# Layer 0 begun on half of the features' modulation, the value projection first in each layer, and a rotation by shuffle

## What is computed

```python
c_act = jax.nn.silu(c)
for l in range(DEPTH):                                  # 2 layers, x is 256 x 1024
    mod = c_act @ w_ada[l] + b_ada[l]                   # 1024 -> 3 x 1024
    shift, scale, gate = split(mod)
    h = rms_norm(x, g_pre[l]) * (1.0 + scale) + shift
    (cq, ckv, kr, za, qb_, kb_, vb_, zb, qc, kc, vc, zc, gcols) = split_cols(h @ w_in[l], IN_SPLITS)
    ...                                                 # three attention branches, gates, output projections
    x = x + gate * rms_norm(y, g_post[l])
# second block
q_rot = axial_rope(q, row_pos, col_pos)                 # x1*cos - x2*sin, x1*sin + x2*cos, halves of 16
k_rot = axial_rope(k, row_pos, col_pos)
...
x = x + gt2 * rms_norm_2(ec_moe(h2, ...))               # 16 experts, each 3 x 1024 x 2752 weights
```

## Time and profile before

| | |
|---|---|
| median of 3 runs | 2330.5 us (2327.39 to 2331.14) |
| profiled execution | 2329.22 us, span 2327.4 us |
| PE busy | 1809.7 us (78%) |
| DVE, ACT, POOL busy | 523.9, 287.3, 61.8 us |
| moved | 714.39 MB, mean 307 GB/s |

### The profile page before, as it was taken

One profiled execution on the slowest core, in us unless ns is written; L12 is line 12 of the kernel. 1 busy time (PEld: TensorE's weight loads), 2 busy tenths in 40 slices (PEclk: granted clock), 3 DMA queues, 4 the chain that ended last, 5 costly groups with the idle time before them and its releaser, 6 DMA issues.

```text
span 2327.4 us, 23978 instructions
## 1 busy us (share of the span) xinstructions
PE 1809.7 (78%) x10388; PEld 1019.3 (44%) x10388; DVE 523.9 (23%) x1136; ACT 287.3 (12%) x710; POOL 61.8 (3%) x101
## 2 busy tenths in 40 slices
PE   6999999999999999989666566656665666666666
PEld 3877785877785677545222222212221222222222
DVE  1144322144323347743000010000100000000001
ACT  1122201122211112311000000000000000000001
POOL 1000000000002100100000000000000000000000
PEclk9999999999999999999777787877787877788787
DMA  9664543445554331388999999999999999999996
GB/s 302 196 203 173 210 147 101 150 163 181 213 180 145 111 124 45 127 331 350 428 426 427 428 429 427 426 430 428 428 425 429 427 427 427 429 427 428 428 428 273
DMA packets 126224, 714.39 MB, mean 307 GB/s; under 512 B 11545, under 2 KB 16089, under 8 KB 96303
## 3 DMA queue, kind: packets, MB, share of 16 engines
q1 hardware_dynamic: 117568, 697.07, 73.9%
q10 hardware_dynamic: 6279, 9.88, 1.4%
q0 software_dynamic: 2272, 5.90, 1.2%
HBM read 709.02 MB, written 3.80 MB: 306 GB/s over the span
## 4 chain that ended last, share of the span: by engine, by line
PE 49%; DMA 44%; DVE 3%; SPq 1%; ACT 1%; issue 1%; POOL 0%; DVEq 0%; ACTq 0%
DMA arena<-in_w_up_dram 22%; DMA arena<-in_w_down_dram 21%; PE banks L832 14%; PE banks L2546 5%; PE banks L1722 4%; PE banks L920 4%; PE banks L1731 3%; PE banks L928 2%; PE banks L2578 2%; DMA arena<-in_w_mods_dram 2%; PE banks L2586 2%; PE banks L837 2%; PE banks L948 1%; PE banks L1764 1%; PE banks L888 1%; PE banks L976 1%
## 5 line engine op out<-in xcount | busy, mean ns | idle before, releaser
L2546 PE MATMUL banks<-arena 128*32 128x512 f32 (+2 forms) x3072 | 418.6, 682 | 330.6 <-DMA arena<-in_w_up_dram 330.6
L2546 PEld LDWEIGHTS banks<-arena 128*32 128x32 f32 x3072 | 131.4, 132 | 588.5 <-issue 580.9
L832 PE MATMUL banks<-arena 128*128 128x256 f32 x1536 | 343.4, 380 | 0.0
L832 PEld LDWEIGHTS banks<-arena 128*128 128x128 f32 x1536 | 287.3, 190 | 39.7 <-issue 3.0
L2578 PE MATMUL banks<-arena 128*32 128x512 f32 x1280 | 206.9, 798 | 92.4 <-DMA arena<-in_w_down_dram 92.4
L2674 DVE SCALAR_TENSOR_TENSOR arena<-arena,banks 64x512 f32<-64x512 f32 (+1 forms) x48 | 30.5, 635 | 519.1 <-ACT arena L2597 518.1
L2578 PEld LDWEIGHTS banks<-arena 128*32 128x32 f32 x1280 | 44.6, 133 | 228.7 <-DMA arena<-in_w_down_dram 128.4
L2597 ACT ACTIVATE arena<-banks 64x512 f32<-64x512 f32 (+1 forms) x48 | 26.7, 556 | 821.1 <-PE banks L2546 819.8
L1722 PE MATMUL banks<-arena 128*128 128x256 f32 x512 | 113.7, 380 | 1.4 <-DVE arena L2119 0.7
L1722 PEld LDWEIGHTS banks<-arena 128*128 128x128 f32 x512 | 95.9, 190 | 16.1 <-issue 3.8
L2681 DVE COPY arena<-banks 128x512 f32<-128x512 f32 x16 | 11.1, 692 | 348.6 <-PE banks L2587 348.6
(11 more groups left out here) (334 smaller groups left out, 1691.1 us busy)
## 6 DMA issues: line engine op xcount, KB each, us to landing
arena<-in_w_gate_dram SPq DMA_DIRECT2D x60, 2752.0 KB, 35.7
arena<-in_w_up_dram SPq DMA_DIRECT2D x60, 2752.0 KB, 32.7
arena<-in_w_down_dram SPq DMA_DIRECT2D x64, 2048.0 KB, 32.4
arena<-in_w_in_dram SPq DMA_DIRECT2D x68, 1024.0 KB, 7.5
arena<-in_w_mods_dram SPq DMA_DIRECT2D x48, 1024.0 KB, 7.4
arena<-in_w_down_dram SPq DMA_DIRECT2D x32, 1024.0 KB, 27.0
arena<-in_w_out_dram SPq DMA_DIRECT2D x12, 1024.0 KB, 5.4
arena<-in_w_gate_dram SPq DMA_DIRECT2D x8, 1376.0 KB, 10.2
```

Of the source, the lines that this page charges most:

```text
L832: mm = pe.matmul(b[:, i * S:i * S + S], w, rhs[:, kt, :], start=kt == 0, stop=kt == 7)
L2546: mm = pe.matmul(bank[pc][32 * g:32 * g + 32, 0:w_], xsT[:, kt, CAP * e4:CAP * e4 + CAP], (wg if g < 2 else wu)[:, c:c + w_], start=kt == ...
```

## The change

- **Half of the features first.** Of layer 0's modulation, blocks 0 and 2 (shift and scale of the features 0 to 511) are made as before. Blocks 1 and 3 are no longer products: VectorE multiplies each row tile by its entry of c and adds, four steps of 128x512 per load (`MODS_B`), and PE adds over the partitions by eight thin products with ones. PE transposes x early into four other banks, without modulation (`turned`). hT's tiles 0 to 3 are written first, and PE makes the first four of eight steps of `vc`, `cq` and the latent keys; the rest of them follows when tiles 4 to 7 are there.
- **Order.** In both layers `vc` is the first job, then `cq`, then the latent keys, which now go to bank SB[0] with signals of their own; the loads are ordered accordingly.
- **Transfers.** x is loaded by SyncE, ahead of the modulation weights. The constants come in two parts: the angle tables of the first rotation are a load of ScalarE's own between the copies of `vc` and `cq`. GpSimd loads the bias tables when VectorE has summed all of `MODS_B`; the T5 product stands between the second halves of `cq` and of the latent keys, `bias_tables(0)` behind the first `qb`.
- **Between the layers.** x of the first half of the tokens is transposed ahead of the last `wout` job, and `vc` begins before the second half of the tokens is scaled; its transposes stand behind seven of the eight steps of the first `vc` job. Fillers go.
- **Second block.** `rk` and `rq` go. VectorE swaps the halves by a shuffle within 32 partitions, and the sine table carries the sign. `gate2` stands ahead of `tq`.

```diff
-    chunk("w_in", D, 0, 416)
+    for r in (0, 512):
+        loads.append(("w_in", r, 4, COL["vc"], 512))
+        loads.append(("w_in", r, 4, 0, 416))
...
-FIRST_MODS = [("ada", 0), ("ada", 1), ("modT", 0), ("ada", 2), ("modT", 1), ("ada", 3), ("modT", 2), ("modT", 3)]
+FIRST_MODS = [("ada", 0), ("ada", 2), ("modT", 0), ("modT", 2)]
...
+MODS_A, MODS_B = (0, 1, 2, 3), (5, 6, 8, 9)
+EARLY = {0: 4, 1: 7}
...
+            sp.dma_start(xv, A["x"][0].rearrange("(t p) d -> p t d", p=P)).then_inc(x_in, 16)
+            for n, turn in enumerate(MODS_A):
+                first_mods(turn, (0, 2)[n // 2], n % 2)
+            load(0, 0)
+            first_mods(MODS_B[0], 1, 0)
+            sp.wait_ge(job_done.sem, made(0, FIRST_MODS.index(("ada", 0)) - PRE))
+            first_mods(MODS_B[1], 1, 1)
+            load(0, 1)
+            sp.wait_ge(job_done.sem, made(0, FIRST_MODS.index(("ada", 2)) - PRE))
+            first_mods(MODS_B[2], 3, 0)
+            first_mods(MODS_B[3], 3, 1)
...
+                if l == 0:
+                    front, back = range(4), range(4, 8)
+                    x_columns(0, 1)
+                    diff_values(0, front)
+                    x_columns(0, 2)
+                    diff_values(1, front).then_inc(part_done.sem, part_done.up())
+                    latent_queries(front)
+                    latent_keys(front).then_inc(part_done.sem, part_done.up())
+                    for n in range(2):
+                        pe.wait_ge(sum_read.sem, sum_read.at(0, 2 * n + 2))
+                        for i in range(4):
+                            mm = pe.matmul(mod_cols[:, 4 * n + i:4 * n + i + 1], th[:, 512 * n + i * P:512 * n + i * P + P],
+                                           ones[:, 0:1], start=True, stop=True)
+                    mm.then_inc(part_done.sem, part_done.up())
+                    x_columns(0, 3)
+                    diff_values(0, back)
+                    x_columns(0, 4)
+                    diff_values(1, back)
+                    latent_queries(back)
+                    pe.wait_ge(tables_in, 160)
+                    pe.matmul(MB[0:12, :], TAB[0:33, 0:12], T5[0:33, :], start=True, stop=True).then_inc(pro_pe.sem, pro_pe.up())
+                    latent_keys(back)
+                else:
+                    x_columns(l, 2)
+                    diff_values(0, range(7))
+                    for hf in range(2):
+                        turned(l, 1, hf)
+                    diff_values(0, range(7, 8))
+                    x_columns(l, 4)
+                    diff_values(1, range(8))
+                    latent_queries(range(8))
+                    latent_keys(range(8))
...
                 act.wait_ge(lam_sum.sem, lam_sum.at(l, 1))
                 nc.scalar.activation(lam[:, 2:4], lam[:, 0:2], ACT.Exp).then_inc(lam_exp.sem, lam_exp.up())
+                for t in range(2):
+                    j = JOB_OF["vc", t]
+                    copy_job(j, vcv[:, t, :], bank_of(l, j))
+                if l == 0:
+                    act.dma_start(cst[:, ANGLES:NCONST[0]], A["consts"][:, ANGLES:NCONST[0]]).then_inc(const_in, 16)
                 j = JOB_OF["cq", 0]
                 copy_job(j, cq, bank_of(l, j))
                 act.dma_start(row_b, A["b_ada"][l:l + 1, 2 * D:3 * D].to_broadcast([P, D])).then_inc(rows_in, 16)
                 act.dma_start(row_g, A["g_post"][l:l + 1, :].to_broadcast([P, D])).then_inc(rows_in, 16)
-                j = JOB_OF["ckv", 0]
-                act.wait_ge(job_done.sem, made(l, j))
-                nc.scalar.copy(ckv, bank_of(l, j)[:, 0:S])
+                act.wait_ge(ckv_done.sem, ckv_done.at(l, 1))
+                nc.scalar.copy(ckv, SB[0][:, 0:S])
...
+            pool.wait_ge(sum_read.sem, sum_read.at(0, 4))
             pool.dma_start(TAB[0:33, 0:12], A["t5_tab"]).then_inc(tables_in, 16)
...
+            for n, turn in enumerate(MODS_B):
+                s_, acc = turn % RING, th[:, 512 * (n // 2):512 * (n // 2) + 512]
+                dve.wait_ge(ring_full[s_], 16 * (turn // RING + 1))
+                for k in range(4):
+                    w, cond = ring[:, s_, 512 * k:512 * k + 512], cav[:, 4 * (n % 2) + k, 0:1]
...
+                        ins = nc.vector.scalar_tensor_tensor(acc, w, cond, acc, ALU.mult, ALU.add)
...
+                    if j == NJOB - 1 and l + 1 < LAYERS:
+                        for hf in range(2):
+                            turned(l + 1, 0, hf)
...
-    jobs += [("rk", n, ()) for n in range(2)] + [("nv", n, i["vn"]) for n in (2, 3)]
-    jobs += [("tq", n, i["qn"]) for n in range(2)] + [("gate2", n, ()) for n in range(2)]
-    jobs += [("rq", n, ()) for n in range(2)]
+    jobs += [("nv", n, i["vn"]) for n in (2, 3)]
+    jobs += [("gate2", n, ()) for n in range(2)] + [("tq", n, i["qn"]) for n in range(2)]
...
+                    nc.vector.stream_shuffle(half, raw, SWAP).then_inc(own2.sem, own2.up())
+                    nc.vector.tensor_tensor(turned, view(raw, 2, S), two(C("cosna")), ALU.mult)
+                    dve.wait_ge(own2.sem, own2.last())
+                    nc.vector.tensor_tensor(tmp, tmp, two(C("sinna")), ALU.mult).then_inc(own2.sem, own2.up())
+                    dve.wait_ge(own2.sem, own2.last())
+                    nc.vector.tensor_tensor(turned, turned, tmp, ALU.add).then_inc(turned2.sem, turned2.up())
```

More of the change, by code:

```diff
@@ L245, in shape_constants @@
     parts["half"] = np.full((P, 4), -0.5, np.float32)
-    later["rot128"] = rotation(P, 16)
+    parts["cos32"] = np.concatenate([cos, cos] * 4).astype(np.float32)
+    parts["sin32"] = np.concatenate([-sin, sin] * 4).astype(np.float32)
     invd = np.float32(10000.0) ** (-np.arange(0, 32, 2, dtype=np.float32) / np.float32(32))
@@ new lines, in _ @@
+            first_mods(MODS_B[0], 1, 0)
[5 more added lines that the diff above has]
+            first_mods(MODS_B[3], 3, 1)
+            for l in range(LAYERS):
+                for i in range(2 if l == 0 else 0, NLOAD):
+                    if l == 0 and i < 8:
+                        if turn_of(0, i) - RING in MODS_B:
+                            sp.wait_ge(sum_read.sem, sum_read.at(0, MODS_B.index(turn_of(0, i) - RING) + 1))
+                        else:
+                            sp.wait_ge(part_done.sem, part_done.at(0, 1 if turn_of(0, i) - RING == EARLY[0] else 2))
+                    elif i - RING in GATE_LOADS:
@@ L1284, in _ @@
                                             ALU.add).then_inc(reader(0, j), 1)
-                if (kind, c) == ("modT", 0):
-                    for t in range(2):
-                        x_mean(0, t)
-                    for t in range(2):
-                        x_scale(0, t)
+            dve.wait_ge(lv_in, 16)
+            for c in (0, 2):
+                j = FIRST_MODS.index(("modT", c)) - PRE
+                dve.wait_ge(reader(0, j), taken(0, j))
+            first_half(0, mcols[:, 0:48].rearrange("p (a b c) -> p a b c", a=2, b=8)[:, :, 0:4, 0])
+            for n, turn in enumerate(MODS_B):
[3 more added lines that the diff above has]
+                    w, cond = ring[:, s_, 512 * k:512 * k + 512], cav[:, 4 * (n % 2) + k, 0:1]
+                    if n % 2 == 0 and k == 0:
+                        ins = nc.vector.tensor_scalar(acc, w, cond, None, ALU.mult)
+                    else:
+                        done = sum_read if k == 0 else sum_own
+                        dve.wait_ge(done.sem, done.last())
+                        ins = nc.vector.scalar_tensor_tensor(acc, w, cond, acc, ALU.mult, ALU.add)
+                    done = sum_read if k == 3 else sum_own
+                    ins.then_inc(done.sem, done.up())
+            dve.wait_ge(part_done.sem, part_done.at(0, 3))
+            first_half(1, view(mod_cols, 2, 4))
             for l in range(LAYERS):
@@ L1525, in _ @@
                         gated(l, t, c, j)
+                        if t == 1 and l + 1 < LAYERS:
+                            dve.wait_ge(ab_ready.sem, ab_ready.at(l + 1, 1))
+                            for hf in range(2):
+                                x_column(l + 1, 0, hf, hf + 1)
                     dve.wait_ge(ysq.sem, ysq.at(l, 2 * t + 2))
@@ L1537, in _ @@
                     x_scale(l + 1, t)
+                if l + 1 < LAYERS:
+                    for hf in range(2):
+                        x_column(l + 1, 1, hf, hf + 3)
                 leave("dve")
```

304 lines of the change are left out of this document (161 added, 143 removed).

## The result

The changed kernel takes **2309.33 us** (median of 4 runs, 2307.18 to 2313.62) against 2329.36 (4 runs, 2327.39 to 2331.14) on the same chip: the ratio of after to before is 0.9920, 95% interval 0.9908 to 0.9932, so 20.0 us faster. The forecast was 2318, range 2305 to 2325. The profiled execution took 2310.95 us with a span of 2309.1, against 2329.2 and 2327.4 before: 18.3 us between the two spans.

The account below looks back on a forecast made before the run. TensorE's chain was taken to bound the kernel until about 1100 us, then the expert weight stream. Layer 0 +1.3, hand-over +6.2 and second block +4.2 sum to 11.7 us: 2318 us against the 2330.5 median, range 2305 to 2325.

Parts of the forecast that it names:

- the hang: Start of layer 0: ScalarE's second load held until 11.1 us behind the T5 write's issue; norm product 8.0 later; chance 0.42.
- rival 1: Start of layer 0: ScalarE's loads pass as in layer 1, gain 21.8 us, time 2308.7; chance 0.27.
- 1.7 of slow clock: Layer 0, behind the held load: 1.7 us counted for TensorE's slow clock after 9 us of idleness.
- Rival 2: Start of layer 0: only ScalarE's third load waits, for 4 us, no slow clock; 5.6 better than forecast, 2312; chance 0.17.
- B: Time at which the back half of layer 0's start begins on TensorE: forecast 40.2 us, bounds 37.5 and 42.
- rival 3: TensorE stays at 1.2 GHz through layer 0's front half, perhaps the queries' products too: 2333 to 2345; chance 0.05.
- The bias rows: Layer 0's first attention step: scores come before the skewed bias load has landed, VectorE stalls; -1.6 us (0 to -3).
- the hand-over: Between the layers: early transposes, and values begun before the second half of x is scaled; +6.2 us (4 to 7).
- the second block's start: Shuffle for rotation products, gate products ahead of queries: scores 4.1 us behind queries instead of 8.25; +4.2 (2 to 5).
- rival 4: Bias load late by the whole 12.6 us, or T5 tables miss their 2.6: up to 4 us more, 2322; chance 0.09.
- one for one: From about 1100 us the expert weight stream's length is fixed by bytes, so time saved before it moves the end equally.
- from there on both traces must be parallel: After the hand-over between the layers, both traces keep their distance, the expert stretch as long as before to 1 us.

Follow-up runs that it names:

- run 5: Changed kernel with ScalarE's two broadcast row loads issued between the key copies and the squares; 2318.54 us, ratio 0.9960 to the kernel before.
- Run 2: Changed kernel with five idle products of 256 columns on TensorE around the second four thin products; 2312.20 us, ratio 0.9927 to the kernel before.
- Run 3: Changed kernel with GpSimd's four skewed bias loads waiting for product qc 1 instead of kc 0; 2307.57 us, ratio 0.9907 to the kernel before.
- run 7: Changed kernel with layer 1's values not begun in the hand-over's wait, nine idle products in their place; 2320.30 us, ratio 0.9970 to the kernel before.
- run 1: Changed kernel with the second block's rotation by four products again, gate products behind the queries, no shuffle; 2315.84 us, ratio 0.9943 to the kernel before.
- run 6: Changed kernel with GpSimd's T5 write issued only when ScalarE's squares are done; 2311.12 us, ratio 0.9928 to the kernel before.
- run 4: Changed kernel with ScalarE's two broadcast row loads issued behind the squares instead of ahead of the key copies; 2310.50 us, ratio 0.9918 to the kernel before.
- run 11: The changed kernel unedited, measured again on the chip of the combined edits; 2310.73 us, ratio 0.9929 to the kernel before.
- run 9: Changed kernel with idle products around the thin products, bias loads behind qc 1 and T5 write behind the squares; 2309.19 us, ratio 0.9918.
- run 10: Changed kernel with the three edits of run 9 and idle products in two more late places; 2305.41 us, ratio 0.9903 to the kernel before.

## Why the prediction was right, and where it was not

**Right in sign and in range, the forecast 8.7 us too high, with the wrong case taken.** The range covered both the hang and no hang, so that the time lies in it says nothing for the hang, and that it lies within 0.7 us of rival 1 is partly luck, as shown below. The step that failed is the hang, as I put it: "If the second load hangs to the same point, 11.1 us behind the write's issue" (-8.0), with 1.7 of slow clock behind it. Measured: the hold, at the third load, ended at 59.34, 3.2 behind the write's issue, and 0.53 us of it reached TensorE. Three things were wrong in that step. I took the end of the hold for a point tied to the write, while the three cases of loads issued 3.9 to 6.9 us behind it show a length of 4.2 to 4.3 us. I had written that the loads go out when the write is just beginning, but did not draw from it that they might be nearly through the queue before its packets run: the last was issued 1.1 us behind the write's issue. And for support I read the earlier trace rows, where 52 to 54 us show only the write's packets; from 49.5 to 52 ScalarE's queue had moved 36 packets beside it. The hold itself is real; run 5, with the load 3.9 us behind the write's issue, pays 7.9. There the clock's part was 3.7 behind 4.6 us of idleness, where I had put 1.7 behind 9 us.

Rival 2 had the mechanism nearest to what the runs show: only the third load waits, and for a length of 4 us. In the changed kernel the length was 2.08. Its time, 2312, counts neither the losses of clock nor that only 0.53 us would show. The sum has a slip as well: 2330.5 less 11.7 is 2318.8, not 2318.

**Rival 1 (no hang, 2308.7) has the right time for the wrong reasons.** Its layer 0 was +11.4; the trace has +5.1. Between them stand the hold's visible 0.5, B and small things 0.3, and two losses:

- The slower clock of the back half, 3.1 us. I had weighed the clock for the front half (rival 3; the front ran at 7.13, so that rival was wrong) and behind the hang, not for the 3.5 us between the halves, in which TensorE ran only the thin products. Run 2 shows the cause: with idle products there the loss was gone in three of three runs, without them in one of eight profiles (run 5). The Trainium skill (TensorE: Matmul & The Clock Gate, Part 1) says that the slow state returns after idling; the traces agree in that, 10.20 against 7.13 us, though here TensorE was not wholly idle.
- The bias rows: forecast 1.6, measured 4.05. The wait itself was 2.3, inside its 0 to 3; the 1.7 of slower clock behind a 2.16 us wait were missing from the sum. Run 3 shows the wait's part; the clock's part came in five of nine profiles with such a wait.

Of these 6.3 us, 4.5 came back elsewhere, which is what brought the time near rival 1's: 0.3 in the hand-over (6.5 for 6.2; run 7), 0.5 in the second block's start (4.7 for 4.2; run 1), 2.0 behind it, and 1.7 by which the medians differ more than the two profiled executions. Another 1.1 is the base: 2330.5 by three runs in the forecast, 2329.36 by four here. Against the forecast's 11.7 the trace has 16.3 at 815 us.

**Held as written:** B at 40.45 (40.2); sums 3.1 behind the last load instead of 2.7; values 1 begin 8.3 us behind the last output product (8.5); first scores 3.5 behind the queries (4.1); VectorE's first bias step waits for the transfer, 6.19 us; the T5 tables did not come late (no wait ahead of the T5 product at 54.04), so that half of rival 4 fell. In the expert stretch, from the first down load (1097.33 and 1079.38) to the end, 1230.1 and 1229.7 us: one for one, in these two traces. **Not held:** "from there on both traces must be parallel" for the 280 us ahead of it, where short waits cost clock.

## What to carry to other kernels

Price a wait of TensorE with the clock behind it, not with its length alone: waits or near-idle stretches of 1.6 to 4.6 us cost 1.4 to 3.7 us on top here. The ones of 1.6 to 2.4 us cost it only in some executions, the 3.5 us in seven of eight profiles, and there idle products took it away in three of three. When an issue was seen blocked beside another queue's transfer, find out first whether the block is a length or a point and where the other transfer's packets begin. A gain of a few microseconds early on is only worth what is left of it at the last wait, so follow a place late in the kernel as well.

## What the runs showed of the hardware

ScalarE's queue is held by GpSimd's write of 768 KB in short rows (run 6 against runs 4 and 5), and the transfers beside it are slow. The transfers view of the changed kernel, 50 to 75 us (KB each, median us from issue to landing):

```profile
t_rows<-arena POOLq DMA_DIRECT2D x1, 768.0 KB, 12.5
arena<-in_b_ada_dram ACTq DMA_DIRECT2D x1, 512.0 KB, 13.0
arena<-in_g_post_dram ACTq DMA_DIRECT2D x1, 512.0 KB, 16.2
```

In layer 1, without the write, the g_post load landed in 4.9 us. SyncE's load of 1024 KB from the same stretch took 16.3. From 62 to 64 us the write moved 0.15 MB in 36 packets, and these took 71.8% of the 16 engines' time; ScalarE's queue had 28 packets and SyncE's 51. The Trainium skill (DMA: Bandwidth & Descriptors, queues and rings) says that a DMA engine takes turns between queues at packet boundaries. Packets of all three queues in this window fit that, but from 52 to 54 us of the kernel before only the write's ran, with ScalarE's load still waiting. Why the issue is held, and why it is the second load's, no run shows.

The clock at a place is not fixed by the code ahead of it. The 16 value records of the back half, with identical code around them, took 10.20 (first profile), 10.11 (run 1), 8.83 (runs 3, 4, 6, 11), 8.72 (run 7) and 7.13 us (run 5). With idle products around the thin products they took 7.13 in all three runs (2, 9, 10). The changed kernel's own runs spread from 2307.2 to 2314.2 us, and a difference of 2 us between two kernels' single profiles says little until the same place has been compared in several.
